# Large expert items of an MoE decoder trunk: gate and up by rows of 14 KB into seven PSUM banks, and another place for the turns of the hidden chunks

## The reference

```python
def moe_swiglu(h, router, w_gate, w_up, w_down):
    tok = h.reshape(B * S, D)
    logits = (tok @ router).astype(jnp.float32)
    top_v, top_i = lax.top_k(logits, TOP_K_EXPERTS)
    w = jax.nn.softmax(top_v, axis=-1)
    gates = jnp.sum(jax.nn.one_hot(top_i, N_EXPERTS) * w[..., None], axis=1)
    for e in range(N_EXPERTS):
        out = out + gates[:, e:e + 1] * (silu(tok @ w_gate[e]) * (tok @ w_up[e])) @ w_down[e]
```

## Time and profile before

| | us |
|---|---|
| median of 3 runs | 1269.29 |
| the profiled execution, its own time | 1269.83 |
| its span, first to last instruction | 1268.1 |
| PE (TensorE) busy in the span | 1234.1 (97%) |
| DVE (VectorE) busy | 637.3 (50%) |
| ACT (ScalarE) busy | 565.2 (45%) |
| DMA, all of it, mean rate | 424.48 MB, 335 GB/s |

### The profile page before, as it was taken

How to read it: one execution, slowest core, us unless ns; L and a number is a source line. 1 busy time by engine, 2 the same in 40 slices (tenths; PEclk the granted TensorE clock), 3 DMA queues, 4 the chain that set the end, 5 groups by cost and what they waited for, 6 DMA issues and landing times.

```text
span 1268.1 us, 18552 instructions
## 1 busy us (share of the span) xinstructions
PE 1234.1 (97%) x7266; PEld 875.2 (69%) x7266; DVE 637.3 (50%) x755; ACT 565.2 (45%) x871; POOL 99.5 (8%) x260
## 2 busy tenths in 40 slices
PE   9998999999999999999999999999999999999787
PEld 8988999999989944588853468884347887332232
DVE  6887765555765501488831168880226886010001
ACT  6665554443655511477730167770036775010001
POOL 1000000000000183100002100000310000110000
PEclk9999999999999999999999999999998999999999
DMA  9943544348533399999999999999999999999997
GB/s 329 373 139 129 199 173 173 122 166 264 194 117 117 134 425 428 403 412 416 428 423 426 421 407 415 416 426 423 428 407 412 415 424 384 423 429 423 426 429 293
DMA packets 89032, 424.48 MB, mean 335 GB/s; under 512 B 5457, under 2 KB 24050, under 8 KB 71282
## 3 DMA queue, kind: packets, MB, share of 16 engines
q1 hardware_dynamic: 88592, 422.76, 83.4%
q10 hardware_dynamic: 354, 0.54, 0.1%
HBM read 422.23 MB, written 1.05 MB: 334 GB/s over the span
## 4 chain that ended last, share of the span: by engine, by line
PE 87%; DMA 8%; DVE 2%; ACT 1%; SPq 1%; issue 1%; ACTq 0%; POOLq 0%; POOL 0%; DVEq 0%
PE psA L2067 9%; PE psY L2082 7%; PE psA L1694 7%; PE psB L2067 7%; PE psA L1696 7%; PE psA L1695 7%; PE psB L1694 7%; PE psB L1696 7%; PE psB L1695 7%; PE psY L1696 5%; PE psY L1695 5%; PE psY L1694 5%; DMA ring<-in_moe_w_gate 3%; DMA ring<-in_moe_w_up 2%; DMA ring<-in_moe_w_down 2%; PE psY L2035 1%
## 5 line engine op out<-in xcount | busy, mean ns | idle before, releaser
L1560 DVE TENSOR_TENSOR wlo<-ring,whi 128x2048 fp32r<-128x2048 f32 (+1 forms) x138 | 287.7, 2104 | 88.3 <-ACT whi L938 86.0
L938 ACT CAST whi<-ring 128x1024 fp32r<-128x1024 f32 x252 | 260.4, 1052 | 100.8 <-issue 34.6
L1307 DVE TENSOR_TENSOR wlo<-ring,whi 128x1024 fp32r<-128x1024 f32 (+2 forms) x104 | 152.3, 1484 | 19.4 <-ACT whi L754 19.3
L2067 PE MATMUL psA<-ring,resT 128*64 128x512 f32 x620 | 148.8, 597 | 13.2 <-DMA ring<-in_moe_w_gate 6.7
L754 ACT CAST whi<-ring 128x1024 fp32r<-128x1024 f32 (+1 forms) x134 | 133.4, 1023 | 60.4 <-PE psY L1696 28.2
L1625 DVE TENSOR_TENSOR rowbuf<-psY,rowbuf 128x512 f32<-128x512 f32 x28 | 18.6, 688 | 211.9 <-PE psY L2035 211.9
L2067 PE MATMUL psB<-ring,resT 128*64 128x512 f32 (+1 forms) x624 | 113.9, 486 | 0.0
L1694 PE MATMUL psA<-xhi,whi 128*128 128x256 f32 x368 | 105.0, 285 | 2.6 <-DVE wlo L1307 1.2
L1694 PE MATMUL psB<-xhi,whi 128*128 128x256 f32 x368 | 106.4, 289 | 0.0
L2067 PEld LDWEIGHTS psB<-ring,resT 128*64 128x64 f32 x624 | 44.9, 137 | 89.0 <-issue 89.0
L1695 PE MATMUL psA<-xlo,whi 128*128 128x256 f32 x368 | 102.8, 279 | 0.0
(11 more groups left out here) (364 smaller groups left out, 2148.3 us busy)
## 6 DMA issues: line engine op xcount, KB each, us to landing
ring<-in_moe_w_down SPq DMA_DIRECT2D x50, 2048.0 KB, 19.9
ring<-in_moe_w_gate SPq DMA_DIRECT2D x35, 1792.0 KB, 10.8
ring<-in_moe_w_up SPq DMA_DIRECT2D x32, 1792.0 KB, 17.7
ring<-in_moe_w_gate SPq DMA_DIRECT2D x18, 2048.0 KB, 20.1
ring<-in_moe_w_up SPq DMA_DIRECT2D x18, 2048.0 KB, 21.4
ring<-in_ffn_w_gate SPq DMA_DIRECT2D x5, 2048.0 KB, 7.8
ring<-in_ffn_w_up SPq DMA_DIRECT2D x5, 2048.0 KB, 8.0
ring<-in_ffn_w_down SPq DMA_DIRECT2D x5, 2048.0 KB, 7.9
```

The lines of the kernel that those rows point to most:

```text
L938: nc.scalar.copy(hi_of(NG + m, 2), item_part(ring, j, g, 2)).then_inc(hi_done, 2)
L1307: nc.vector.tensor_tensor(part_of(wlo, s, g, size), part_of(ring, s, g, size), f(hi_of(m, size)), ALU.subtract).then_inc(lo_done, size)
L1560: nc.vector.tensor_tensor(item_part(wlo, j, g, step), item_part(ring, j, g, step), f(hi_of(NG + m, step)), ALU.subtract).then_inc(lo_done, ...
L2067: ins = mm(few_bank(b)[half * FEW:(half + 1) * FEW, to:to + end - x], few_in[:, k, :], raw[:, x - q * W:end - q * W], start=k == 0, stop=k ...
```

## The change

Large items take the small items' order of loads: `item_slots` is now one table for both, 8 slots of gate, 8 of up (7 groups each, one block of 128 input rows, all 3584 columns), 7 of down. The first two loads are cut into three parts (2, 2, 3 and 3, 2, 2 groups). Gate gathers in seven PSUM banks (`big_bank`), then SiLU is applied bank by bank, up gathers in the same banks, and down's result goes to `psA`, the banks of chunks 0 and 1. The activations lie in `hidT`, `squares_of` and `resT` (`big_act`). Chunks 0 and 1 are turned within up's last slot, behind its fourth and fifth group; chunk c+1 ahead of the fifth group of down's slot c, for c from 1 to 5. Since 7 groups don't divide into twos and fours, and pieces end at slots, at the ends of ring slots and of `whi`, ScalarE now casts in 92 pieces per item (84 before) and VectorE subtracts in 57 (46 before). The low parts of down's first twelve groups stand ahead of the products of chunks 2 and 3 or between them; after that VectorE is twelve groups ahead of a slot's end. The small items' banks change their order, and an item behind a large one waits at its third bank for the large one's result.

```diff
         return 1 if m < single else 4 if m in ffn_groups and slots[group_of[m][0]][1] == GS else 2
 
 
-    item_slots = [("gate", 0, 1, 0), ("up", 0, 1, 0)]
-    for c in range(1, NE, 2):
-        item_slots += [(kind, c, 2, part) for kind in ("gate", "up") for part in range(2)]
-        item_slots += [("down", d, 1, 0) for d in range(max(c - 2, 0), c)]
-    item_slots += [("down", d, 1, 0) for d in range(NE - 2, NE)]
-    item_slot = {key: j for j, key in enumerate(item_slots)}
-    PAIRED = [(0, 1)] + [(c, 2) for c in range(1, NE, 2)]
-    IS = len(item_slots)
...
+    BIG_FROM = GS * ((NS + SHIFT) % RING)
+
+    def split_pieces(first_size, size):
+        pieces, m = [], 0
+        for j in range(FS):
+            end = item_from[j] + item_cells[j]
+            while m < end:
+                n = min(first_size if j < 2 else size, end - m, HL - (NG + m) % HL, GS - (BIG_FROM + m) % GS)
+                pieces.append((m, n))
+                m += n
+        return pieces
+
+    HI_PIECES, LO_PIECES = split_pieces(2, 2), split_pieces(2, 4)
...
+            return (psB[:, 0, :], psB[:, 1, :], psA[:, 1, :], psA[:, 0, :])[b][:, 0:BANKS[b]]
+
+        def big_bank(c):
+            return (psA[:, 0, :], psA[:, 1, :], psB[:, 0, :], psB[:, 1, :], psY[:, 1, :], psY[:, 2, :], psY[:, 0, :])[c]
+
+        def big_act(c):
+            if c < 4:
+                t = hidT[:, :, :].rearrange("p b n -> p (b n)") if c < 2 else squares_of
+                return t[:, c % 2 * W:c % 2 * W + W]
+            return blocks(resT, 2 * (c - 5), 2) if c > 4 else blocks(resT, KD - 2, 2)
...
+                for j, (kind, at) in enumerate(item_slots):
+                    sp.reg_add(used_past, used_past, item_cells[j])
+                    sp.wait_ge(group_used, used_past)
                     if kind == "down":
-                        src = moe_w_down[0][e, c * W:(c + 1) * W, :].rearrange("(p g) n -> p (g n)", p=P)
-                    else:
-                        w, rows = moe_w_gate if kind == "gate" else moe_w_up, D // wide
-                        src = w[0][e, part * rows:(part + 1) * rows, c * W:(c + wide) * W].rearrange("(k p) n -> p k n", p=P)
-                    dst, landed = ring[ring_at(i, j)][:, :], slot_full[ring_at(i, j)]
-                    if len(src.shape) == 3:
-                        dst = dst.rearrange("p (k n) -> p k n", n=src.shape[2])
-                    sp.reg_add(used_past, used_past, GS)
-                    sp.wait_ge(group_used, used_past)
+                        src = moe_w_down[0][e, at * W:(at + 1) * W, :].rearrange("(p g) n -> p (g n)", p=P)
+                        sp.dma_start(few_runs(i, j)[0][0], src).then_inc(item_full[j], 16)
+                        continue
+                    w = moe_w_gate if kind == "gate" else moe_w_up
+                    src = w[0][e, at * P:(at + 1) * P, :]
                     if j < 2:
-                        for a in range(GS // 2):
-                            ks = slice(2 * a, 2 * a + 2)
-                            sp.dma_start(dst[:, ks, :], src[:, ks, :]).then_inc(
-                                first_full[j][a] if a < GS // 2 - 1 else landed, 16)
-                    else:
-                        sp.dma_start(dst, src).then_inc(landed, 16)
+                        to, q = few_runs(i, j)[0][0], 0
+                        for a, n in enumerate(FIRST_PARTS[j]):
+                            sp.dma_start(to[:, q * W:(q + n) * W], src[:, q * W:(q + n) * W]).then_inc(
+                                first_full[j][a] if a < len(FIRST_PARTS[j]) - 1 else item_full[j], 16)
+                            q += n
+                        continue
+                    for to, q, n in few_runs(i, j):
+                        sp.dma_start(to, src[:, q * W:(q + n) * W]).then_inc(item_full[j], 16)
...
-                done = AHEAD
-                for j in range(IS):
-                    stop = min(GS * (j + 1) + AHEAD + 2, IG)
-                    item_split(i, done, stop)
-                    done = max(done, stop)
-                    for c in TURN_AFTER.get(j, []):
-                        hidden_hi(i, c)
-                    if j in GATE_END:
-                        act.wait_ge(group_used, used_at(i, GS * (j + 1)))
-                        c, wide = GATE_END[j]
-                        for d in range(c, c + wide):
-                            nc.scalar.activation(in_blocks(hid_of(d)), by_block(psA[:, half_of(d), :]), ACT.Silu).then_inc(m_silu, 1)
+                done = sum(1 for m, size in HI_PIECES if m < NE)
+                for k in range(KD - 1):
+                    done = item_split(i, done, item_from[k + 1] + AHEAD + 2)
+                for c in range(NE):
+                    act.wait_ge(group_used, used_at(i, item_from[KD - 1] + c + 1))
+                    nc.scalar.activation(in_blocks(big_act(c)), by_block(big_bank(c)), ACT.Silu).then_inc(m_silu, 1)
+                    done = item_split(i, done, item_from[KD - 1] + c + 1 + AHEAD + 2)
+                for k in range(KD - 1):
+                    done = item_split(i, done, item_from[KD + k + 1] + AHEAD + 2)
+                done = item_split(i, done, 2 * CELLS + 4)
+                hidden_hi(i, 0)
+                done = item_split(i, done, 2 * CELLS + GS)
+                hidden_hi(i, 1)
+                for d in range(NE):
+                    done = item_split(i, done, 2 * CELLS + GS * (d + 1) + AHEAD + 6)
+                    if d + 2 < NE:
+                        hidden_hi(i, d + 2)
...
+            def multiply(i, c):
+                dve.wait_ge(group_used, used_at(i, item_from[2 * KD - 1] + c + 1))
+                dve.wait_ge(m_silu, i * NE + (c + 1))
+                nc.vector.tensor_tensor(in_blocks(big_act(c)), by_block(big_bank(c)), in_blocks(big_act(c)),
+                                        ALU.mult).then_inc(m_hid, 1)
 
             def expert(i):
-                done = AHEAD
-                for j in range(IS):
-                    stop = min(GS * (j + 1) + AHEAD, IG)
-                    item_halve(i, done, stop, 4 if j else 2)
-                    done = stop
-                    for c in TURN_AFTER.get(j, []):
-                        hidden_lo(i, c)
-                    if j in UP_END:
-                        dve.wait_ge(group_used, used_at(i, GS * (j + 1)))
-                        c, wide = UP_END[j]
-                        for d in range(c, c + wide):
-                            dve.wait_ge(m_silu, i * NE + (d + 1))
-                            nc.vector.tensor_tensor(in_blocks(hid_of(d)), by_block(psB[:, half_of(d), :]), in_blocks(hid_of(d)),
-                                                    ALU.mult).then_inc(m_hid, 1)
+                done = sum(1 for m, size in LO_PIECES if m < NE)
+                for j in range(2 * KD - 1):
+                    done = item_halve(i, done, item_from[j + 1] + AHEAD)
+                multiply(i, 0)
+                multiply(i, 1)
+                done = item_halve(i, done, 2 * CELLS + 4)
+                hidden_lo(i, 0)
+                hidden_lo(i, 1)
+                done = item_halve(i, done, 2 * CELLS + GS)
+                multiply(i, 2)
+                done = item_halve(i, done, 2 * CELLS + GS + 4)
+                multiply(i, 3)
+                for d in range(NE):
+                    done = item_halve(i, done, 2 * CELLS + GS * (d + 1) + AHEAD + 4)
+                    if d + 2 < NE:
+                        hidden_lo(i, d + 2)
+                    if d + 4 < NE:
+                        multiply(i, d + 4)
...
+                    if kind == "gate" and k == 0 and b == 2 and isinstance(i, int) and i:
+                        pe.wait_ge(y_out, 2 * i)
...
-            def item_slot_products(i, j):
-                kind, c, wide, part = item_slots[j]
-                if kind == "gate" and c and part == 0:
-                    pe.wait_ge(m_silu, i * NE + c)
-                if kind == "up" and c and part == 0:
-                    pe.wait_ge(m_hlo, hlo_at(i, c - 1))
-                if kind == "down" and c == 0:
-                    pe.wait_ge(y_out, 2 * i)
-                if kind == "down":
-                    pe.wait_ge(m_hlo, hlo_at(i, c))
+            def big_columns(i, j, kind, k):
+                if kind == "gate":
+                    pe.wait_ge(ilo_done, ilo_at(i, k))
+                for c in range(NE):
+                    m = item_from[j] + c
+                    if m in LO_AT:
+                        pe.wait_ge(lo_done, split_at(i, m + LO_AT[m]))
+                    if j == 0 and c == 5:
+                        pe.wait_ge(ilo_done, ilo_at(i, KD // 2 - 1))
+                        pe.wait_ge(few_rows_set, few_at(i + 1))
+                    if j == 0 and c == NE - 1:
+                        pe.wait_ge(y_out, 2 * i)
+                    if kind == "up" and k == 0:
+                        pe.wait_ge(m_silu, i * NE + (c + 1))
```

(65 more changed lines are left out.)

133 lines of the change are left out of this document (66 added, 67 removed).

## The result

| | before | after |
|---|---|---|
| median of 8 runs each, us | 1268.59 (1267.65 to 1269.39) | 1272.14 (1270.45 to 1273.41) |
| ratio, 95% interval | | 1.0026 (1.0015 to 1.0036) |
| profiled execution, us | 1269.83 | 1272.29 |
| its span, us | 1268.1 | 1270.5 |

The account below looks back on a forecast made before the run. DMA and PE both run near their limit; with the ring full, PE's end of the last large item sets the time. New waits 9.9, kept 0.5, removed 8.2: +2.2 us on 1269.29, so 1271.5; range 1264 to 1277, own range 1268 to 1273.

Parts of the forecast that it names:

- The three new waits: PE in each large item: 0.7 us at group 64, 1.0 at chunk 0's turn, 1.6 at down's start; 9.9 in all.
- point 4: In down, a turn and four groups cover the copy and product: no wait; VectorE has 5.96 us of PE's 6.04 a slot.
- the costs of 0 for more pieces and for SyncE: More low parts and casts, 1.7 us more on VectorE, stay under PE's 121 us; SyncE's issue costs nothing.
- Waits that go: Start of the second and third large items: PE's waits for the third load, 2.26 and 5.97 us, 8.2 together, go.
- I kept 0.5 us in all: Start of the third large item: group 20 lands 0.4 to 0.9 us late, so 0.5 us of the old wait stays.
- The frame: Ring full at the last large item's end, so PE's shift of that moment is the change in time.
- The loads: I put it at 0: Wider rows in large items save 3.1 us each, 9.3 over three, but count 0 beside the full ring.
- my rival of 1261.1 us: No new waits reach PE, the old 8.2 us go: 1261.1 us, with half the new waits 1266; chance 0.22.
- the rule of few bytes: Skill's fixed overhead per packet: rows of 2, 4 and 14 KB should load alike; the trace differs by 4 to 8%.
- New waits stay off PE: SiLUs and copies overlap casts more than expected: 1261.1 us without new waits, 1266 with half; chance 0.22.
- The waits at the start of L items stay: Third load of the second and third large items still late, up to 8.2 us: 1274 to 1279 us; chance 0.25.
- The rows don't get wider in effect: Loads cut where the ring wraps: 3.1 us shrink to some 2, time changes under 0.5 us; no separate chance.

Follow-up runs that it names:

- e8_before_again: The kernel before the change, unchanged, profiled once more: 1268.36 us in one execution.
- e1_copy: The kernel after, with ScalarE's copy of chunk 1 ahead of the casts of groups 116 to 119: 1270.65 us, ratio 1.0014 to the kernel before.
- e2_product: The kernel after, with VectorE's products of chunks 0 and 1 ahead of the low parts of groups 112 to 115: 1268.81 us, ratio 1.0004 to the kernel before.
- e6_low64: The kernel after, with the low parts of groups 64 to 67 in two pieces of two: 1270.39 us, ratio 1.0013 to the kernel before.
- e3_joints: The kernel after, with copy and products moved ahead, low parts at 64 and 112 split, chunks 0 and 1 turned one group earlier: 1262.74 us, ratio 0.9958.
- e4_third: The kernel before, with the third load of large items in two parts, a semaphore each: 1268.00 us, ratio 0.9997.
- e5_narrow: e3_joints, with gate and up loads from the third on cut into pieces of two groups, rows of 4 KB: 1268.03 us, ratio 0.9994 to the kernel before.
- e7_fourth: The kernel before, with the third and fourth loads of large items in two parts each: 1268.43 us, ratio 0.9997.

## Why the prediction was right or wrong, point by point

The forecast was +2.2 us, 1271.5; measured are 1272.14 us and a difference of 3.3 to 3.6 us (by ratio, by medians). The time lies in the forecast's own range, but the effect is larger by half, and falls beyond the 0.2% within which I had put most of its chance. That the time came so close is in part luck: the median of 3 from which I started, 1269.29 us, was 0.7 us above the median of 8, and +2.2 us on the latter would have been 1270.8 us. The mechanism came true: new waits on PE that outweigh the old ones, with L items forecast at 124.6 us and measured at 124.30 to 124.85 us.

- **The three new waits: right in place and cause, a little too large.** Predicted 0.7, 1.0 and 1.6 us, 3.3 an item; measured 0.46, 0.88 and 1.40, with the slower steps behind them 3.00. Each went with one edit. The hop-by-hop clock held: counted from the start of group 103 (601.72 us), PE was to turn chunk 0 at 5.17 and to start down at 9.7 us; it did so at 5.07 and 9.51. The 0.1 us for hand-overs at group 64 was not needed.
- **In down, no wait (point 4): right**, in all three items. The S item (86.65 us) is right too, and for the costs of 0 for more pieces and for SyncE no wait on PE speaks against them.
- **"Waits that go": the term that was mis-sized most.** I took 8.2 us. In e8_before_again, an execution at the median, they are 2.16 + 4.68 = 6.8 us. Of the 1.4 us between, 1.3 are the third L item, in the stretch at the lower clock: the waits themselves were alike (3.04 and 3.00 us), what followed was not. One execution is no measure of such a term.
- **The rest of them.** I kept 0.5 us in all; it is 0.53 in item 3 and 0.55 in item 5, 1.1 us, so 0.6 too little where the new waits were 0.9 too much. With it the waits that come are 3.00 + 3.53 + 3.55 = 10.1 us, where I had 10.4; less 6.8 this is +3.3 us, the measured difference.
- **The frame, that the shift of the last L end is the shift of the time: right where the ring is full there.** After against e8_before_again: 1076.23 - 1072.93 = +3.3 us, the times of these two executions being 3.9 us apart; against the page before the shift is 1.9 us, the times 2.5. Over before, after, e8_before_again, e1_copy, e2_product, e6_low64 and e3_joints the rest is 193.4 to 194.9 us, so the rule is good to 1.5 us, which is half of this effect. Where the ring isn't full, in e4_third, e5_narrow and e7_fourth, the rest is 195.9 to 197.2 us and the rule fails. The prediction said that PE waits in two places only; that is so within the L items, but in every kernel here it also waits for loads in item 7, 14.0 us in all by the brackets in the page before and 14.3 in the one after. The chain that ends last in the kernel after runs there on the loads, from 1156.17 us on: (its row `1156.17 25.32 DMA ring<-in_moe_w_gate`). As I read it, the end is set by loads that start from a full ring, and so it moves with the moment at which the ring is full for the last time.
- **"The loads: I put it at 0": right for this comparison, incomplete as a picture.** PE's new waits set when the ring is full for the last time, so the faster loads gave nothing. But I read the full ring of the earlier trace rows as room. There was hardly any: without PE's old waits the kernel before would have met a bound by its loads at 1268 us, which my rival of 1261.1 us didn't know. The wide rows lift that bound by at least 4.6 to 5.3 us (e5_narrow against e3_joints, by ratios and by medians); how far exactly is open, since in e3_joints the ring still fills (328 GB/s at 640 us). So of the two things that the change does, the rows are worth some 5 us once PE lets them, and the new order on ScalarE and VectorE costs 8.6 to 9.4 us against the mended one, which e3_joints shows is not the price of the wide rows.
- **The width of rows against the rule of few bytes.** The runs confirm: 405 GB/s with 4 KB rows and 423 with 14 KB in the same stretch of two kernels with the same orders on PE, ScalarE and VectorE. The Trainium skill (DMA: Bandwidth & Descriptors, "Why small descriptors are slow") has a fixed overhead of about 3 cycles per packet beside one per 32 bytes. I took this as no difference at these widths; worked out from its figures with a row as one packet, an estimate, rows of 4 KB take 131 cycles for 128 of data and rows of 14 KB 451 for 448, which is 1.7% apart. Measured are 4%, so the direction agrees and the size does not.
- **The rivals.** "New waits stay off PE" fell, all three are there. "The waits at the start of L items stay" fell: items 3 and 5 lost only 0.27 and 0.30 us in brackets there, so the third load lands in time to about half a microsecond. "The rows don't get wider in effect" fell by the packets and the rate.

## What to carry to other kernels

Where a compute engine and the loads take turns at the limit, look for both bounds before costing a change that lifts one: a full buffer at the end says who sets the time now, not how much there is to win. A new order of work has to be read at its joints, on each in-order engine: a bulk cast or subtraction that is written ahead of the one small copy or product that PE waits for costs PE a good part of its length (0.88 us of a subtraction of 2.29 here, 1.40 us of casts of 2.00). Moving that one line brings back what the next joint leaves of it: all of it at the turn of chunk 0, some 0.4 us of 1.40 at down's start. And a term that is a wait plus what the clock does behind it should be measured in more than one execution.

## What the hardware showed that was not expected

- Rows of 4 KB load 4% slower than rows of 14 KB (405 and 423 GB/s, e5_narrow and e3_joints at 560 us), and between these two kernels that was 4.6 to 5.3 us of 1268.
- After nearly the same idle time of PE, 3.04 and 3.00 us, two executions of one kernel differ in how much of the next 10 us runs at the lower level (granted clock 0.66 and 0.83 of 2.4 GHz, the lower level being 1.2 GHz). Behind an idle time of 1.85 us at 958.82 in e4_third, and of 2.04 us at 750.35 in the kernel before, the clock was 1.00 for the item.
- A wait of PE costs more than the idle time: the first matmul behind it takes 0.34 us to the next instead of 0.23 at group 64 and at down's start; at the turn, where transposes stand first, it is 0.05 us.
